# Small loads one stage later, solved blocks read before the fox norms, and four heads of the first branch chunk multiplied ahead of the fox stage

## The reference

```python
proj = rmsnorm(x, g_mix) @ w_in                  # one projection, 6680 columns
# fox attention, 8 heads of 64: softmax(q k / 8 + c_q - c_k, causal) v, c = cumsum(log forget)
q, k = rmsnorm(fq), rmsnorm(fk);  y_a = fox_attend(q, k, fv, c)
# gated delta net, 8 heads: causal conv of width 4 (with 3 rows of history), l2norm, chunks
a = I + strict(kb k^T * decay);  u, w = solve(a, [v * beta, k * beta * exp(G)])
v_new = u - w S;  o = (q exp(G)) S + attn v_new;  S = S * g_last + k_dec^T v_new
y_b = rmsnorm(o, g_onorm) * silu(z)
x1 = x + (sig(g_a) * (y_a @ w_br_a) + sig(g_b) * (y_b @ w_br_b)) @ w_out
x2 = x1 + hier_moe(rmsnorm(x1))                  # 32 experts, top 2 in one group
```

## Time and profile before

| | us |
|---|---|
| median of three runs | 1282.86 |
| the profiled execution's own time | 1283.12 |
| its span, from first to last instruction | 1281.3 |
| TensorE busy | 1104.4 (86%) |
| VectorE, ScalarE, GpSimd busy | 418.0, 356.1, 384.5 |
| start of the second stage's first matmul | 31.37 |
| first matmul of the delta net's first tile | 292.68 |
| first matmul of the fox stage | 456.59 |
| mean granted TensorE clock | 0.942 |

### The profile page before, as it was taken

One profiled execution on the slowest core, in us unless ns is written; L12 is line 12 of the kernel. 1 busy time (PEld: TensorE's weight loads), 2 busy tenths in 40 slices (PEclk: granted clock), 3 DMA queues, 4 the chain that ended last, 5 costly groups with the idle time before them and its releaser, 6 DMA issues. The chain is left out here.

```text
span 1281.3 us, 20377 instructions
## 1 busy us (share of the span) xinstructions
PE 1104.4 (86%) x8218; PEld 846.2 (66%) x8218; DVE 418.0 (33%) x931; ACT 356.1 (28%) x747; POOL 384.5 (30%) x426
## 2 busy tenths in 40 slices
PE   4999899898999979998998978888888777788781
PEld 3998888787998858888996844454444444444440
DVE  5597733881111544331324442210101000000004
ACT  4547633351222734442333330000000000000000
POOL 3554459741212433332553011111211111111100
PEclk9999989987999979999999879989999999988996
DMA  7322236244332511115323959999999999999975
GB/s 124 83 68 66 76 87 173 52 120 129 94 87 72 211 50 50 50 50 193 92 75 104 420 183 361 404 411 396 403 406 406 406 409 406 403 412 409 406 321 214
DMA packets 149145, 284.57 MB, mean 222 GB/s; under 512 B 43988, under 2 KB 119348, under 8 KB 132688
## 3 DMA queue, kind: packets, MB, share of 16 engines
q1 hardware_dynamic: 93072, 242.71, 50.4%
q10 hardware_dynamic: 50256, 29.69, 8.3%
q0 software_dynamic: 5744, 11.15, 2.5%
HBM read 267.08 MB, written 24.31 MB: 227 GB/s over the span
## 5 line engine op out<-in xcount | busy, mean ns | idle before, releaser
L489 PE MATMUL bank<-xhi,cv_w_hi 128*128 128x272 f32 x848 | 260.9, 308 | 11.4 <-PEq L132 6.0
L2482 PE MATMUL bank<-e_w,b_xT 128*64 128x256 f32 x2048 | 235.8, 388 | 34.8 <-DVE b_xT L2509 25.0
L475 POOL TENSOR_TENSOR cv_w_lo<-cv_w_raw,cv_w_hi 128x1024 fp32r<-128x1024 f32 (+1 forms) x69 | 165.8, 2403 | 328.6 <-ACT cv_w_hi L468 328.1
L489 PE MATMUL bank<-xhi,cv_w_lo 128*128 128x272 f32 x848 | 251.5, 297 | 0.0
L489 PE MATMUL bank<-xlo,cv_w_hi 128*128 128x272 f32 x848 | 251.2, 296 | 0.0
L2482 PEld LDWEIGHTS bank<-e_w,b_xT 128*64 128x64 f32 x2048 | 147.3, 139 | 113.3 <-DVE b_xT L2509 30.4
L489 PEld LDWEIGHTS bank<-xhi,cv_w_hi 128*128 128x128 f32 x848 | 166.5, 196 | 19.5 <-issue 11.6
L489 PEld LDWEIGHTS bank<-xlo,cv_w_hi 128*128 128x128 f32 x848 | 167.0, 197 | 1.0
L489 PEld LDWEIGHTS bank<-xhi,cv_w_lo 128*128 128x128 f32 x848 | 166.5, 196 | 0.0
L2494 PE MATMUL bank<-e_w,b_hiddenT 128*64 128x512 f32 x512 | 128.4, 647 | 30.8 <-DVE b_hiddenT L2517 16.3
L2450 POOL COPY b_target<-slot_target 128x1 int32 (+1 forms) x32 | 5.7, 178 | 372.2 <-ACT b_y L2504 372.2
(11 more groups left out here) (436 smaller groups left out, 1625.9 us busy)
## 6 DMA issues: line engine op xcount, KB each, us to landing
e_w<-in_w_e SPq DMA_DIRECT2D x96, 2048.0 KB, 38.1
cv_w_raw<-in_w_in ACTq DMA_DIRECT2D x34, 512.0 KB, 4.1
cv_w_raw<-in_w_in SPq DMA_DIRECT2D x18, 512.0 KB, 3.8
cv_w_raw<-in_w_br_b ACTq DMA_DIRECT2D x8, 512.0 KB, 4.3
o_raw<-in_w_out SPq DMA_DIRECT2D x16, 256.0 KB, 3.7
g_values_gates<-g_z_stage ACTq DMA_DIRECT2D x12, 272.0 KB, 4.4
f_gates<-g_values_gates SPq DMA_DIRECT2D x2, 1088.0 KB, 8.7
x_in<-in_x_prompt SPq DMA_DIRECT2D x4, 512.0 KB, 6.9
```

Of the source, the lines that this page charges most:

```text
L475: self.k.nc.gpsimd.tensor_tensor(self.wlo[:, s, 0:nk, :], self.raw[:, s, 0:nk, :], self.whi[:, c % OPS, 0:nk, :].bitcast(F32), ALU.subtract)\
L489: last = self.k.nc.tensor.matmul(self.bank(c, h)[:, 0:HALF], w, x[:, d, cols], start=(d == 0 and n == 0), stop=(d == nk - 1 and n == 2))
L2482: last = nc.tensor.matmul(k.bank[bank][sl[a], 0:FH], xT[:, d, :], w[slot][:, d, FH * a:FH * a + FH], start=(d == 0), stop=(d == KD - 1))
```

## The change

Three edits in one.

1. `start` no longer loads `hist` and no longer waits for the small loads. The other thirteen raise `small_in`, for which ScalarE waits ahead of L610 and VectorE ahead of L645 in the next stage. There SyncE loads `hist` first, ahead of the weight chunks, and VectorE waits for it ahead of the convolution.
2. `chunk_in` is cut in two, `blocks_of` (the seven reads of solved blocks) and `matrices_of` (the two others). `blocks_of(1)` is issued as soon as the blocks are written back. `matrices_of(1)` waits for the first four fox norms and for the matrices' own write, `matrices_of(2)` for all eight. The halves of the ring are swapped, so that tile 1 has the first half, where the first four roots lie.
3. Of chunk 41, the parts of both halves with d = 0 to 3 are multiplied at the end of `head_rows` (`EARLY_PARTS`, 8 parts) and taken out of the fox stage's `Fill`, which deals 184 parts and not 192. VectorE makes the low parts of heads 0 to 3 earlier, between heads 5 and 6, and no longer that of head 4. GpSimd makes those of heads 4 to 7, the last one behind the first mask.

```diff
-LOW_HEADS = 5
+LOW_HEADS = 4
+EARLY_PARTS = [(BRANCH_B[0], h, d) for h in range(2) for d in range(LOW_HEADS)]
@@ start: sync
-                for w in range(3):
-                    loads.append((k.hist[:, w, :], i["state_gdn_conv"][0, 0, w].rearrange("(c p) -> p c", p=128)))
                 for dst, src in loads:
-                    sp.dma_start(dst, src).then_inc(loaded, 16)
-            sp.wait_ge(loaded, 16 * len(loads))
+                    sp.dma_start(dst, src).then_inc(k.small_in, 16)
+                k.small_loads = 16 * len(loads)
@@ convolved_projections: sync, scalar, vector
+                    for w in range(3):
+                        sp.dma_start(k.hist[:, w, :], k.i["state_gdn_conv"][0, 0, w].rearrange("(c p) -> p c", p=128))\
+                            .then_inc(k.hist_in, 16)
                 for j in range(RAWS, NCC + 1):
                     s.load(sp, j)
...
+                a.wait_ge(k.small_in, k.small_loads)
                 c_(nc.scalar.activation(k.sm_coef[64:72, :], k.sm_coef[64:72, :], ACT.Exp))
...
+                v.wait_ge(k.small_in, k.small_loads)
                 for h in range(2):
                     v.wait_ge(s.half, h + 1)
...
+                v.wait_ge(k.hist_in, 48)
                 for c in range(NCC):
@@ delta_net
-        mt = lambda t, h: chunk_ring[:, t % 2, 0, h, :]
+        mt = lambda t, h: chunk_ring[:, (t + 1) % 2, 0, h, :]
...
-                sp.wait_ge(norms.scaled, 8)
+                sp.wait_ge(back, 32)
+                sp.wait_ge(zeroed, 2)
+                blocks_of(1)
                 for s in A:
                     for a in A:
                         sp.wait_ge(at_out[s][a], 32)
-                sp.wait_ge(back, 32)
-                sp.wait_ge(zeroed, 2)
-                chunk_in(1)
-                chunk_in(2)
+                sp.wait_ge(norms.scaled, 4)
+                matrices_of(1)
+                blocks_of(2)
+                sp.wait_ge(norms.scaled, 8)
+                matrices_of(2)
@@ head_rows: tensor (end), vector (end)
+            for c, h, d in EARLY_PARTS:
+                pe.wait_ge(low, d + 1)
+                s_.part(pe, c, h, d)
...
-            for x in ("k0", "k1", 0, 1, 2, 3, "k2", "k3", 4, 5, "k4", 6, 7):
...
-            for h in range(LOW_HEADS):
...
+            for t in (0, 1):
+                keep_keys(t)
+            for h in range(4):
+                gated(h)
+            for t in (2, 3):
+                keep_keys(t)
+            for h in (4, 5):
+                gated(h)
+            low_part(0)
+            low_part(1)
+            keep_keys(4)
+            low_part(2)
+            low_part(3)
+            for h in (6, 7):
+                gated(h)
@@ fox_heads
-    fill = Fill(s_, range(BRANCH_B[0], BRANCH_B[7] + 1), even(12 * 2 * KD, [f"{x}{j}" for j in range(J + 2) for x in "ab"]))
+    fill = Fill(s_, range(BRANCH_B[0], BRANCH_B[7] + 1), even(12 * 2 * KD - len(EARLY_PARTS), [f"{x}{j}" for j in range(J + 2) for x in "ab"]),
+                EARLY_PARTS)
...
+            for h in range(LOW_HEADS, H - 1):
+                low_part(h)
+            mask(0)
+            low_part(H - 1)
             for j in range(J + 2):
-                if j < J:
+                if 1 <= j < J:
                     mask(j)
```

More of the change, by code:

```diff
@@ L244, in start @@
     junk, rt, rr = k.junk, stat[:, 1], stat[:, 2]
-    filled, loaded, ints, done, early = (k.sem("const_" + n) for n in ("filled", "loaded", "ints", "done", "early"))
+    filled, ints, done, early = (k.sem("const_" + n) for n in ("filled", "ints", "done", "early"))
+    k.small_in, k.hist_in = k.sem("small_in", k.top), k.sem("hist_in", k.top)
     x_loaded = [k.sem(f"x_loaded{t}") for t in range(5)]
@@ L500, with __init__ @@
 class Fill:
-    def __init__(self, stream, chunks, points):
+    def __init__(self, stream, chunks, points, done=()):
         self.nk, self.n = lambda c: stream.chunks[c][1], len(stream.chunks)
-        todo = [(c, h, d) for c in chunks for h in range(2) for d in range(self.nk(c))]
+        todo = [(c, h, d) for c in chunks for h in range(2) for d in range(self.nk(c))
+                if (c, h, d) not in done]
         assert sum(points.values()) == len(todo), (sum(points.values()), len(todo))
@@ L569, in _ @@
             def _(sp):
+                with nc.allow_non_contiguous_dma(reason="small parameters"):
+                    for w in range(3):
+                        sp.dma_start(k.hist[:, w, :], k.i["state_gdn_conv"][0, 0, w].rearrange("(c p) -> p c", p=128))\
+                            .then_inc(k.hist_in, 16)
                 for j in range(RAWS, NCC + 1):
@@ L842, in _, with blocks_of @@
             def _(sp):
-                def chunk_in(t):
-                    us = slice(8 * (t - 1), 8 * t)
+                def blocks_of(t):
                     if t >= 3:
@@ L903, in _ @@
                     if t == 0:
-                        chunk_in(3)
-                        chunk_in(4)
+                        blocks_of(3)
+                        matrices_of(3)
+                        blocks_of(4)
+                        matrices_of(4)
                 sp.wait_ge(loaded, 32)
@@ L1519, in head_rows @@
                                    "gate", "hi"))
+    low = k.sem("f1_low")
     z_in, k_out = [k.sem(f"f1_z_in{s}") for s in range(2)], [k.sem(f"f1_k_out{s}") for s in range(2)]
@@ L1622, in _, with low_part @@
             last.then_inc(restc, 1)
-            for x in ("k0", "k1", 0, 1, 2, 3, "k2", "k3", 4, 5, "k4", 6, 7):
[L1624 to L1627, removed]
-            for h in range(LOW_HEADS):
-                v.wait_ge(hi, h + 1)
-                nc.vector.tensor_tensor(k.ybl[:, h, :], k.yb[:, h, :], k.ybh[:, h, :].bitcast(F32), ALU.subtract)
+            def low_part(h):
+                v.wait_ge(hi, h + 1)
+                nc.vector.tensor_tensor(k.ybl[:, h, :], k.yb[:, h, :], k.ybh[:, h, :].bitcast(F32), ALU.subtract).then_inc(low, 1)
+            for t in (0, 1):
[13 more added lines that the diff above has]
+                gated(h)
         @block.scalar
@@ L1718, in mask, with low_part @@
                     .then_inc(masked, 1)
-            for h in range(LOW_HEADS, H):
+            def low_part(h):
                 nc.gpsimd.tensor_tensor(k.ybl[:, h, :], k.yb[:, h, :], k.ybh[:, h, :].bitcast(F32), ALU.subtract).then_inc(low_heads, 1)
+            for h in range(LOW_HEADS, H - 1):
+                low_part(h)
+            mask(0)
+            low_part(H - 1)
             for j in range(J + 2):
-                if j < J:
+                if 1 <= j < J:
                     mask(j)
```

8 lines of the change are left out of this document (5 added, 3 removed).

## The result

The changed kernel took 1269.49 us (median of four runs, 1267.22 to 1272.19), where the kernel before took 1282.76 (1282.11 to 1283.66): a ratio of 0.9899, 95% interval 0.9881 to 0.9918, or 13.0 us (10.5 to 15.3). Forecast were 1264.2 and 18.7 us less. With six more runs on another chip (e5) the ratio was 0.9895 (0.9860 to 0.9930). The time lies at the upper edge of the range (1269.8), and close to what rival (a) gave, 1269.2.

What follows compares the result with a forecast made beforehand. The expert stage ends last and starts when the TensorE work ahead allows. Gains of 4.0, 11.8 (hole 6.8, clock 5.0) and 2.9 sum to 18.7 us: 1264.2 on the median's scale, range 1260 to 1269.8.

Steps and rivals of the forecast that it cites:

- rival (a): Delta net: the clock is not kept, only the hole goes; 5.0 us less gain, 1269.2 us; chance 0.14.
- Bound: Expert stage ends last and its loads wait for TensorE matmuls, so a microsecond saved ahead moves the end by one.
- Part 1: Small loads at the first stage's end: 4.0 us gained, from 3.0 to 4.5.
- The boundary: First to second stage: TensorE ends the stage, 1.51 us of idle instead of 4.54; 3.0 us gained.
- The clock: Second stage's start: TensorE's clock stays fast behind the shorter gap; 1.0 us gained, between 0 and 1.5.
- The wait for GpSimd's low part: Second stage: TensorE waits for the next weights' low part, ready 3.5 us after the start, limiting the clock's gain to 1.5.
- Part 2, the hole: Ahead of the delta net's tile 1: earlier reads remove 6.8 of 7.17 us idle, leaving 0.4.
- Rival (b): Ahead of tile 1: the matrices land 2.8 us late; 2.8 or 7.8 us less gain, 1267 to 1272; chance 0.06.
- Part 2, the clock: Delta net's tile 1: work starts before the clock falls and runs fast to its cross product; 5.0 us gained, 0 at least.
- Part 3: Fox stage: 24 matmuls moved into the 7.04 us hole ahead; 2.9 us gained, from 1.5 to 6.
- (c): Fox stage doesn't give its 3.0 us, since TensorE waits for the softmax chain; 1267.2 us; chance 0.09.
- (e): Slower: the clock stays down after tile 1's new start, costing 19 us over one tile; 1288 us; chance 0.02.

Runs made afterwards that it cites:

- e5: The changed kernel run once more, unaltered, beside the kernel before on another chip: 1268.35 us, ratio 0.9895 to the kernel before.
- e2: The kernel before with only the early reads of solved blocks (second edit): ratio 0.9927 to the kernel before, -9.4 us.
- e6: The changed kernel with each tile's 24 small joined-block products in two loops by weight width, not in turns head by head: 1255.83 us, ratio 0.9790 to the kernel before.
- e3: The kernel before with only the four heads multiplied ahead of the fox stage (third edit): ratio 0.9989 to the kernel before, -1.4 us.
- e8: The changed kernel with one extra 272-column matmul behind each head of the joined blocks: ratio 1.0023 to the kernel before.
- e9: The kernel before with the joined blocks in two loops, without any part of the change: 1269.94 us, ratio 0.9917 to the kernel before.
- e10: The kernel before with the joined blocks in two loops and its hole ahead of tile 1 filled by 52 matmuls: ratio 0.9885 to the kernel before.
- e11: The kernel of e6 run once more, beside e9 and e10 on the same chip: 1255.45 us, ratio 0.9800 to the kernel before.
- e4: The changed kernel with three filling parts (9 matmuls) dealt between each tile's small joined-block matmuls: ratio 0.9936 to the kernel before.
- e12: The kernel of e6 with tile 1's two matrix reads behind four of its seven block reads, not all: 1255.16 us, ratio 0.9800 to the kernel before.

## Why the prediction was right and wrong

**Bound.** Right: what was saved ahead of the expert stage reached the end, -14.0 at the mixed stage and -14.5 at the span (-16.8 and -17.2 in e5).

**Part 1.** 4.0 us forecast. The boundary gave 4.0 of its own (forecast 3.0: TensorE ended the stage at 26.42, and the barrier cost 0.97, where 1.51 had been taken from another one). The clock added 1.3 by the delta net's start (1.0 forecast) and 0.4 came up to the solved blocks: 5.7. The wait for GpSimd's low part, which the forecast had, came and was short (0.36 us).

**Part 2, the hole.** 6.8 forecast, 6.6 measured (-5.7 to -12.4), 6.4 in e5. The wait was 1.50 us, not 0.4, since one of the block reads took 1.29 us to issue and not 0.48 (1.5 to 1.7 in e2, e5 and e6); TensorE came earlier too. Rival (b), the late matrices, decided nothing: the last read landed after 5.2 us, for which 5.6 had been taken.

**Part 2, the clock: this is the step that failed.** "TensorE now reaches this work at 285.9, before the fall. Gain 4.9 us, and 0.1 in the cross product itself: 5.0." The size of the prize was right: without a drop tile 1 takes 23.0 us with two loops, so 24.6 with the turns, and 29.66 - 24.6 = 5.1. But it came only by 2.1 us, for the clock fell twice inside the tile, at 281.3 and 288.1, with TensorE busy. The second drop stands behind the joined blocks, and e2, with no idle ahead of the tile, had this one alone: 3.6 us gained. The first one stands 1.0 us behind the 1.50 us of idle that was left, where the prediction had 0.4; it cost the other 1.5, and whether the longer wait brought it about stays open. And tiles 3 and 4, for which no change was forecast, gave 4.4 back in one execution (30.92 and 22.11 for 29.48 and 19.17) and nothing in the other. Over the four tiles the change came to 2.2 us lost in the first trace and 2.1 gained in e5, where 5.0 gained had been forecast. The forecast took tile 2 of one execution, at 1.00, as what a tile does once the hole is gone, and so treated idle as the one thing that lowers the clock. The same trace has two drops with no idle ahead of them, 278.3 to 285.1 and, in tile 3, 356.9 to 360.2, and the prediction weighs neither.

**Part 3.** 2.9 forecast, -10.1 to -14.0 = 3.9 measured, 2.7 in e5, 3.3 in e3. The fox stage itself became shorter by 3.6, 3.9 and 3.8 us, more than the 3.0 of its 24 matmuls: at its start the clock was low for 7.0 us in the changed kernel, 9.5 before, a gain that the prediction named and left out of its sum. The way to it became 0.3 us shorter in the changed kernel, but 1.2 longer in e5 and 0.5 in e3, where 0.1 had been taken. One reason for the difference is that the first trace lacks a drop of 3.4 us, some 16 us behind the last `held_out`, that the kernel before, e3 and e5 all have. The low parts were held beside GpSimd's split, as taken: VectorE and GpSimd in the changed kernel,

```profile
435.68 3.54 DVE L1647 TENSOR_TENSOR yb_lo<-conv_v,yb_hi 128x544 fp32r<-128x544 f32 x2
...
439.75 1.34 DVE L1647 TENSOR_TENSOR yb_lo<-conv_v,yb_hi 128x544 fp32r<-128x544 f32 x2
```

```profile
435.82 2.83 POOL L475 TENSOR_TENSOR cv_w_lo<-cv_w_raw,cv_w_hi 128x1024 fp32r<-128x1024 f32 x1 [2.99 <-ACT cv_w_hi L468]
```

two low parts in 3.54 us with the split beside them, and in 1.34 without. The Trainium skill says on the page SBUF — State Buffer, section SBUF: two separate sides, that a VectorE operation with two SBUF inputs and a GpSimd one that reads SBUF exclude each other for a whole instruction. These rows agree with it: the two low parts end 0.57 us behind the split. TensorE waited 1.4 us for them, within the old hole.

**The rivals.** (a) gave the right time for a reason half right, and partly by luck: most of the clock's 5.0 us were missing in the tiles, but not because the slow stretch stood where it had been. It is the term that (a) doubted, and 0.14 was too little for it. (c) was wrong, the fox stage gave its 3 us. (e), the slower side, had the mechanism in small: a clock that falls in work that ran fast before; it cost 4.4 us in one trace, not 19. What was held against it, that the clock came back after at most 6 us of dense matmuls, says how a drop ends and not whether one comes.

**What stays open.** How the 13.0 us on average split over the executions: two traces of one kernel differ by 2.7 us in span, and only their tiles were followed. e5's trace alone, 17.2 us less in span than the one trace of the kernel before, comes close to the 18.7 forecast, and no median does. That the drops of tiles 2 to 4 come from the joined blocks in turns is shown by the five traces of two loops, which have none; e8's longer stretch and longer drops fit it. What in it counts was not told apart: two loops take away the turns and halve the length. The stretch ahead of tile 1 speaks for the length: it lasts some 4.6 us, changes shape only between its four groups, and has a drop in 9 of 14 traces, among them four of the five of two loops (e6, e9, e10, e11), which are clean in tiles 2 to 4.

## What to carry to other kernels

Full busy time doesn't mean a kept clock: before pricing work at the fast clock, look at every low stretch in the trace, above all those with no idle ahead of them, and count with their turning up elsewhere. Small matmuls that took turns between weight widths were dear twice here, in their own time and in the clock behind them; grouped by shape they took half the time, and that one line was worth nearly as much as the change itself (e6, e11: 1255.5 us, better than both kernels). Matmuls of another shape in between didn't help (e4) or made it worse (e8).

## What the runs showed of the hardware that was not expected

- A change of shape among small matmuls costs about 0.12 us, an estimate from 24 products in 3.3 us with 15 changes and in 1.67 with one.
- One matmul of 272 columns on the whole array costs 0.32 us between small ones and 0.125 among its like.
- TensorE's clock can fall while its busy time is full: behind the turns in tiles 2 to 4 (nine of nine traces) and in the thin stretch ahead of tile 1 (9 of 14).
- One kernel, run twice, drops the clock in different tiles (e5), and a kernel's runs on the later chips spread over some 15 us.
- Reordering nine reads that one queue issues within 7 us didn't move the moment at which the last one has landed (e12).
